# Windowed attention with the values as the stationary operand: the probabilities divided first, the heads left turned, the norm taken by a product with ones

## The reference

```python
lse = jnp.logaddexp(jax.nn.logsumexp(scores, axis=-1), sink)
probs = jnp.exp(scores - lse[..., None])
out = jnp.einsum('bnkgqs,bnskd->bnqkgd', probs, v_band)
...
att = rmsnorm(att, g_att)        # over all 512 attention features of a token
ml = rmsnorm(ml.reshape(b, s, ML_HEADS, ML_V_DIM), ...)
return jnp.concatenate([att, ml], axis=-1) @ w_out
```

## Time and profile before

| | |
|---|---|
| median of 3 runs | 1009.53 us (1009.29 to 1009.66) |
| the profiled execution, its own time | 1009.17 us |
| span of its instructions | 1007.4 us |
| TensorE busy | 997.8 us |
| VectorE busy | 744.7 us |
| ScalarE busy | 505.8 us |
| granted TensorE clock | 0.999 of full |

### The profile page before, as it was taken

How to read it: one execution, slowest core, us unless ns; L and a number is a source line. 1 busy time by engine, 2 the same in 40 slices (tenths; PEclk the granted TensorE clock), 3 DMA queues, 4 the chain that set the end, 5 groups by cost and what they waited for, 6 DMA issues and landing times.

```text
span 1007.4 us, 13062 instructions
## 1 busy us (share of the span) xinstructions
PE 997.8 (99%) x4807; PEld 823.8 (82%) x4807; DVE 744.7 (74%) x1164; ACT 505.8 (50%) x949; POOL 25.9 (3%) x40
## 2 busy tenths in 40 slices
PE   9999999999999999999999999999999999999997
PEld 6788888888888888788888888888888888888886
DVE  4563678875645569997777777777776879996796
ACT  5663448643733225755445445445544634444573
POOL 2000000000300000000000000000000000000000
PEclk9999999999999999999999999999999999999999
DMA  9527554222832241423223223223222999035104
GB/s 343 186 91 224 187 189 168 85 66 108 298 117 84 84 124 51 141 84 105 63 84 104 63 84 104 63 84 100 68 81 81 391 363 336 1 117 190 40 1 167
DMA packets 93255, 133.97 MB, mean 133 GB/s; under 512 B 5884, under 2 KB 56188, under 8 KB 93192
## 3 DMA queue, kind: packets, MB, share of 16 engines
q1 hardware_dynamic: 92808, 132.98, 39.5%
q0 software_dynamic: 96, 0.00, 0.1%
q10 hardware_dynamic: 288, 0.15, 0.1%
HBM read 104.75 MB, written 28.35 MB: 132 GB/s over the span
## 4 chain that ended last, share of the span: by engine, by line
PE 77%; DVE 4%; issue 1%; ACT 0%; DVEq 0%; ACTq 0%
PE pz L2339 7%; PE pz L2340 7%; PE pz L2338 7%; PE pd L2338 6%; PE pd L2339 6%; PE pd L2340 6%; PE pd L2359 4%; PE pd L2362 4%; PE pd L2361 4%; PE pz L2359 3%; PE pz L2362 3%; PE pz L2361 3%; PE pd L2243 3%; PE pd L2245 3%; PE pd L2244 3%; PE pz L2274 1%
## 5 line engine op out<-in xcount | busy, mean ns | idle before, releaser
L1109 ACT ACTIVATE ws_hi<-raw 128x512 fp32r<-128x512 f32 x88 | 52.9, 626 | 102.4 <-PE pz L2340 48.0
L2338 PE MATMUL pz<-ht_hi,ws_hi 128*128 128x512 f32 x240 | 93.7, 390 | 0.2 <-ACT u L1131 0.2
L2340 PE MATMUL pz<-ht_hi,ws_lo 128*128 128x512 f32 x240 | 93.5, 389 | 0.0
L2339 PE MATMUL pz<-ht_lo,ws_hi 128*128 128x512 f32 x240 | 93.4, 389 | 0.0
L2338 PE MATMUL pd<-ht_hi,ws_hi 128*128 128x512 f32 x200 | 78.0, 390 | 0.5 <-DVE u L1792 0.5
L2340 PE MATMUL pd<-ht_hi,ws_lo 128*128 128x512 f32 x200 | 77.9, 389 | 0.0
L2339 PE MATMUL pd<-ht_lo,ws_hi 128*128 128x512 f32 x200 | 77.9, 389 | 0.0
L1809 DVE SCALAR_TENSOR_TENSOR gate<-u,vec,gate 128x1023 f32<-128x1023 f32 (+1 forms) x44 | 56.4, 1283 | 19.4 <-ACT gate L1151 18.6
L1779 DVE TENSOR_TENSOR ws_lo<-raw,ws_hi 128x512 fp32r<-128x512 f32 x88 | 58.5, 686 | 0.8 <-ACT ws_hi L1109 0.7
L1809 DVE SCALAR_TENSOR_TENSOR lift<-u,vec,lift 128x1023 f32<-128x1023 f32 (+1 forms) x44 | 56.2, 1278 | 0.1
L1184 ACT ACTIVATE d_hi<-a 128x512 fp32r<-128x512 f32 x44 | 27.7, 631 | 54.4 <-PE pd L2362 29.6
(11 more groups left out here) (312 smaller groups left out, 2550.8 us busy)
## 6 DMA issues: line engine op xcount, KB each, us to landing
raw<-in_w_up SPq DMA_DIRECT2D x48, 512.0 KB, 5.0
b<-in_w_down SPq DMA_DIRECT2D x49, 256.0 KB, 7.0
act_rows<-gate SPq DMA_DIRECT2D x22, 512.0 KB, 2.6
a<-act_rows SPq DMA_DIRECT2D x44, 256.0 KB, 4.7
w_raw<-in_w_wide SPq DMA_DIRECT2D x16, 512.0 KB, 3.9
x_turned<-in_x_t SPq DMA_DIRECT2D x8, 512.0 KB, 9.5
x_in<-in_x SPq DMA_DIRECT2D x8, 512.0 KB, 12.9
wo_hi_rows<-wo_new_hi SPq DMA_DIRECT2D x8, 512.0 KB, 5.0
```

What stands on the lines that cost most here:

```text
L1109: nc.scalar.activation(ws_hi[m][:, :, :], summand(p, i), ACT.Copy).then_inc(s["ws_hi_made"], 1)
L2338: mm(dst, wh[:, k, :], xh[:, k, :], start=begins and k == 0, stop=False, skip_group_check=not begins)
L2339: mm(dst, wh[:, k, :], xl[:, k, :], start=False, stop=False, skip_group_check=not begins)
L2340: ins = mm(dst, wl[:, k, :], xh[:, k, :], start=False, stop=k == KH - 1, skip_group_check=not begins)
```

## The change

- `attend(n)` takes the values as stationary operand (64 columns for each key/value head) and the turned probabilities as the moving one: two products of 256 columns instead of four of 64. Each writes one half of the partitions; the result has features on the partitions and tokens along the free axis, already turned for the output projection. The rows of `w_out` and of its gain are loaded in the matching order.
- The division by the sum can no longer be made on the result, so ScalarE's `att_p_scale(n)` divides the probabilities (four passes of 128x128) before `turn_probs(n)`, which waits for it; `att_keep(n)` becomes a plain copy.
- `attend(n-4)`, `turn_probs(n-2)` and `attend(n-3)` alternate in step n.
- The norm's sum now runs over partitions. Squares are added pairwise on VectorE (`att_sq_add`, two small sums for a chunk) into one row block, and `att_total` (four products with ones, after `ml_sum(0)`) adds them over the partitions. The root (128x256), its reciprocal on VectorE, a store to memory and a load that spreads it over all partitions follow; VectorE's `att_scale(i)` (128x512) replaces ScalarE's sixteen passes.
- `turn_mix(i)` keeps four of its eight transposes; `mix_high` and `mix_low` work in two halves. `fold` and its three GpSimd instructions are gone. The second tile of the up projection's weights is loaded later.

Left out of this diff: tile and semaphore declarations, waits whose name or count alone changed, the order of `w_out`'s rows.

```diff
@@ -602,8 +601,10 @@
...
             load_gate(0)
-            load_gate(1)
...
+                if i == NT - 1:
+                    sp.wait_ge(s["att_scaled"], NT)
+                    load_gate(1)
@@ -922,14 +916,20 @@
...
+            def att_p_scale(n):
+                _, kw = keys(n)
+                act.wait_ge(s["att_summed"], 2 * n + 2)
+                for j in range(4):
+                    p = probs[:, n % 2, j, 0:kw]
+                    last = nc.scalar.activation(p, p, ACT.Copy, scale=inv[:, n % 4, j:j + 1])
+                last.then_inc(s["att_p_scaled"], 1)
             def att_square(n):
                 act.wait_ge(s["att_kept"], n + 1)
-                if n == 0:
-                    act.wait_ge(s["att_scored"], 5)
-                else:
-                    act.wait_ge(s["att_squared"], n)
-                nc.scalar.activation(att_squares[:, :, :], zq[:, n, :, :], ACT.Square,
-                                     accum_out=sq_att[:, n:n + 1]).then_inc(s["att_squared"], 1)
+                act.wait_ge(s["att_sq_added"], 2 * n)
+                for h, dst in enumerate((att_sq_a, att_sq_b)):
+                    last = nc.scalar.activation(dst[:, :, :], zq[:, n, 2 * h:2 * h + 2, :], ACT.Square)
+                last.then_inc(s["att_squared"], 1)
             def wo_high(k):
@@ -967,9 +967,10 @@
...
                             gate_exps()
-                    for m in (n - 5, n - 4):
-                        if n % 2 == 1 and 0 <= m < NC:
-                            att_square(m)
+                    if 0 <= n < NC:
+                        att_p_scale(n)
+                    if 0 <= n - 5 < NC:
+                        att_square(n - 5)
@@ -993,16 +994,27 @@
...
             def mix_high(i):
-                act.wait_ge(s["mix_turned"], i + 1)
+                act.wait_ge(s["att_scaled"], i + 1)
...
                     act.wait_ge(s["out_done"], 2 * (i - 1))
-                nc.scalar.activation(mix_hi[i % 2][:, :, :].rearrange("p k t -> p (k t)"), pz[1][:, :], ACT.Copy)\
+                nc.scalar.activation(mix_hi[i % 2][:, 0:4, :].rearrange("p j (n t) -> p n j t", n=2),
+                                     zq[:, 2 * i:2 * i + 2, :, :], ACT.Copy).then_inc(s["mix_hi_made"], 1)
+                act.wait_ge(s["mix_turned"], i + 1)
+                nc.scalar.activation(mix_hi[i % 2][:, 4:NK, :].rearrange("p k t -> p (k t)"), bank[2], ACT.Copy)\
...
-            def att_scale(n):
+            def att_root():
+                act.wait_ge(s["att_norm_step"], 1)
+                nc.scalar.activation(att_r[:, :], bank[2][:, 0:2 * P], ACT.Sqrt, bias=eps[:, :],
+                                     scale=1.0 / (ATT_HEADS * HD)).then_inc(s["att_norm_step"], 1)
+            def store_att_row():
...
-                nc.scalar.activation(zq[:, n, :, :], zq[:, n, :, :], ACT.Copy, scale=r_att[:, n:n + 1])\
-                    .then_inc(s["att_scaled"], 1)
+                act.dma_start(att_r_d.rearrange("(g t) -> g t", g=4), att_r[0:P:32, :]).then_inc(s["rows_stored"], 16)
+            def spread_att_row():
+                act.wait_ge(s["rows_stored"], 48)
+                act.dma_start(att_row[:, :], att_r_d.partition_broadcast(P)).then_inc(s["rows_spread"], 16)
             def ml_scale(i):
@@ -1011,12 +1023,12 @@
...
             for i in range(NT):
-                if i == 0:
-                    act.wait_ge(s["att_norm_step"], 1)
-                    nc.scalar.activation(r_att0[:, :], att_sums[:, :], ACT.Sqrt, bias=eps[:, :],
-                                         scale=1.0 / (ATT_HEADS * HD)).then_inc(s["att_norm_step"], 1)
-                    for n in range(4):
-                        att_scale(n)
+                if i == 1:
+                    att_root()
+                if i == 2:
+                    store_att_row()
+                if i == 3:
+                    spread_att_row()
@@ -1024,8 +1036,6 @@
...
                         ml_scale(i - NT + 4)
-                    for n in (2 * i + 2, 2 * i + 3):
-                        att_scale(n)
             def h2_high(i):
@@ -1462,10 +1472,8 @@
...
                     .then_inc(s["att_summed"], 1)
-                dve.wait_ge(s["att_summed"], 3 * n + 1)
-                if n >= 4:
-                    dve.wait_ge(s["att_kept"], n - 3)
-                nc.vector.reciprocal(inv[:, n % 4, :], total1[:, u, :]).then_inc(s["att_summed"], 2)
+                dve.wait_ge(s["att_summed"], 2 * n + 1)
+                nc.vector.reciprocal(inv[:, n % 4, :], total1[:, u, :]).then_inc(s["att_summed"], 1)
             def att_p_keep(n):
@@ -1478,10 +1486,18 @@
             def att_keep(n):
                 dve.wait_ge(s["att_done"], n - n % 2 + 2)
-                dve.wait_ge(s["att_summed"], 3 * n + 3)
-                nc.vector.tensor_tensor(zq[:, n, :, :], bank[7][:, n % 2 * 256:n % 2 * 256 + 256].rearrange("p (j d) -> p j d", j=4),
-                                        inv[:, n % 4, :].unsqueeze(2).to_broadcast([P, 4, HD]), ALU.mult)\
+                c = n % 2 * 256
+                nc.vector.tensor_copy(zq[:, n, :, :], bank[7][:, c:c + 256].rearrange("p (j t) -> p j t", j=4))\
...
+            def att_sq_add(n):
+                dve.wait_ge(s["att_squared"], n + 1)
+                nc.vector.tensor_tensor(att_sq_a[:, :, :], att_sq_a[:, :, :], att_sq_b[:, :, :], ALU.add)\
+                    .then_inc(s["att_sq_added"], 1)
+                dve.wait_ge(s["att_sq_added"], 2 * n + 1)
+                dve.wait_ge(s["att_scored"], min(n + 2, NC))
+                nc.vector.tensor_tensor(z[:, AK, n * CHUNK:(n + 1) * CHUNK], att_sq_a[:, 0, :], att_sq_a[:, 1, :], ALU.add)\
+                    .then_inc(s["att_sq_added"], 1)
             def wo_low(k):
@@ -1580,6 +1596,8 @@
...
                         scale_q((n - 8) // 2)
+                    if 0 <= n - 6 < NC:
+                        att_sq_add(n - 6)
@@ -1591,8 +1609,6 @@
             def ml_carry(i):
                 dve.wait_ge(s["ml_stated"], i + 1)
-                if i == 0:
-                    nc.vector.tensor_copy(att_sums[:, :], bank[7][:, HALF - NC:]).then_inc(s["att_norm_step"], 1)
@@ -1636,7 +1652,13 @@
             def att_norm():
                 dve.wait_ge(s["att_norm_step"], 2)
-                nc.vector.reciprocal(r_att[:, :], r_att0[:, :]).then_inc(s["att_norm_step"], 1)
+                nc.vector.reciprocal(att_r[:, :], att_r[:, :]).then_inc(s["att_norm_step"], 1)
+            def att_scale(i):
+                dve.wait_ge(s["rows_spread"], 16 * 9)
+                v = zq[:, 2 * i:2 * i + 2, :, :]
+                r = att_row[:, i * P:(i + 1) * P].rearrange("p (n t) -> p n t", n=2).unsqueeze(2).to_broadcast([P, 2, 4, CHUNK])
+                nc.vector.tensor_tensor(v, v, r, ALU.mult).then_inc(s["att_scaled"], 1)
             def ml_norm(i):
@@ -1651,9 +1673,12 @@
...
             def mix_low(i):
-                dve.wait_ge(s["mix_hi_made"], i + 1)
-                nc.vector.tensor_tensor(mix_lo[i % 2][:, :, :].rearrange("p k t -> p (k t)"), pz[1][:, :],
-                                        mix_hi[i % 2][:, :, :].rearrange("p k t -> p (k t)").bitcast(F32),
+                dve.wait_ge(s["mix_hi_made"], 2 * i + 1)
+                views = [m[i % 2][:, 0:4, :].rearrange("p j (n t) -> p n j t", n=2) for m in (mix_lo, mix_hi)]
+                nc.vector.tensor_tensor(views[0], zq[:, 2 * i:2 * i + 2, :, :], views[1].bitcast(F32), ALU.subtract)
+                dve.wait_ge(s["mix_hi_made"], 2 * i + 2)
+                nc.vector.tensor_tensor(mix_lo[i % 2][:, 4:NK, :].rearrange("p k t -> p (k t)"), bank[2],
+                                        mix_hi[i % 2][:, 4:NK, :].rearrange("p k t -> p (k t)").bitcast(F32),
...
             def add_x(i, half):
@@ -1726,8 +1751,10 @@
...
                     ml_carry(i + 1)
-                if i == 0:
+                if i == 1:
...
+                if i >= NT - 3 and i < NT - 1:
+                    att_scale(i - NT + 3)
@@ -1738,6 +1765,7 @@
...
                     mix_scale(i + 2)
+                    att_scale(i + 2)
@@ -2108,7 +2136,7 @@
             def turn_probs(n):
                 _, kw = keys(n)
-                pe.wait_ge(s["att_exped"], n + 1)
+                pe.wait_ge(s["att_p_scaled"], n + 1)
@@ -2122,10 +2150,10 @@
...
                 v = att_vb[:, n // 2 - 1, :] if n and n % 2 == 0 else att_va[:, n // 2, :]
-                for j in range(4):
-                    kv = j // 2
-                    ins = mm(bank[7][:, c + j * HD:c + (j + 1) * HD], probs_t[0:kw, n % 2, j, :],
-                             v[0:kw, kv * HD:(kv + 1) * HD], start=True, stop=True)
+                for kv in range(KV_HEADS):
+                    rows = slice(kv * HD, (kv + 1) * HD)
+                    ins = mm(bank[7][rows, c:c + 4 * CHUNK], v[0:kw, rows],
+                             probs_t[0:kw, n % 2, 2 * kv:2 * kv + 2, :].rearrange("k u t -> k (u t)"), start=True, stop=True)
...
             def attention(block):
@@ -2134,13 +2162,12 @@
...
```

(67 more changed lines are left out.)

10 lines of the change are left out of this document (3 added, 7 removed).

## The result

The changed kernel takes 1014.77 us (median of 4 runs, 1014.17 to 1015.42), beside 1009.60 for the kernel before: 1.0048 times as long, 95% interval 1.0036 to 1.0060. The profiled execution took 1014.17, 5.0 more than before; its span is 1012.4. The executions of the kernel before, 1009.29 to 1009.90, and of the changed one do not overlap. I had predicted 1012.7 and slower as the likeliest sign.

What follows compares the result with a forecast made beforehand. TensorE, busy 99% of the span, was taken as the bound. Attention stage +4.8, mLSTM stage +2.0 and `turn_mix` -3.5 gave +3.3 on 1009.17, so 1012.5, stated as 1012.7 us; range 1004.5 to 1015.5.

Steps and rivals of the forecast that it cites:

- the forecast by itself: Whole kernel, the main case: 1012.7 us, by itself 1010.8 to 1014.8; chance 45%.
- TensorE's products: TensorE: two `attend`s take 0.60 us each, saving 0.45 a step; `att_total` adds 0.7, `fold` going saves 0.3.
- the twofold price: `attend` at the skill's 2x speedup: the three steps where TensorE does not wait give another 0.6 us, so 1012.1.
- The weights of step 10: Attention stage: ScalarE's longer chain splits the unit's weights 2.1 to 2.2 us late; 2.1 us lost at step 10.
- Dividing and squares: ScalarE, chunks 7 and 8: four dividing passes (1.26 us) and two squares (0.5), ending at 157.9 and 168.4.
- Step lengths: Attention stage: late copies for `turn_probs` make step 10 last 5.5 us instead of 3.77; steps 12, 14, 16 also lengthen.
- Attention stage: Steps 4 to 18: 6.3 us lost from step 8 to 18, 0.45 won at steps 4 and 6, 0.6 at 18; +4.8.
- mLSTM: mLSTM stage: `ml_state(1)` waits +0.7, wide reciprocal +0.9 or nothing, `att_total` +0.7, `fold` -0.3, `att_scale`s 0; +2.0 us.
- The row: The norm row's store and spread, sharing engines with `w_out`'s loads: taken as 0, up to 7 us if each took 10.1.
- rival 3: Store and spread queue behind `w_out`: 3 to 7 us before mLSTM block 7, 1016 to 1019 us; chance 10%.
- `turn_mix` and the output projection: Four transposes fewer save 0.43 us, eight times, 3.5 in all; output projection's `att_scale` and split are hidden, 0.
- Rivals 1 and 2: Attention stage: slack covers the weights' chain fully (1004.7 us, 20%) or TensorE's losses are about half (1009 to 1010, 25%).

## Why the prediction was right, and where its steps were not

The mechanism came as forecast: TensorE lost its work and got more than that back in waits for w_lo, probs_t and ml_k. The size came at the upper edge, 1014.77 against a band of 1010.8 to 1014.8 for the forecast by itself.

- **TensorE's products.** `attend` 0.58 us, taken as 0.60; steps 4 and 6 won 0.75 and 0.5, taken as 0.45 each. `att_total` 0.64, taken as 0.7. By the Trainium skill (TensorEngine Tiling (Array Packing), "Theoretical Speedup") the swap may be worth up to twofold; this trace shows 0.865 / 0.58 = 1.5, and the first `attend` of a step starts 0.32 us behind the last product of the unit instead of 0.23 (155.54 to 155.86; before, 156.60 to 156.83). The prediction has a slip at the twofold price: three steps that win 0.865 each instead of 0.45, 0.45 and 0.6 give another 1.1, not 0.6, and so 1011.6, not 1012.1.
- **TensorE's busy time** fell by 5.2 us, forecast 6 to 7. At the half clock of step 10 three rows are 0.42, 0.47 and 0.67 us longer than at step 8; without these 1.6 it is 6.8.
- **The weights of step 10.** From the start of step 8 to that of step 10 the changed kernel takes 174.33 - 155.86 = 18.5 us, before 15.0: 3.5 lost, 2.1 forecast. The place, the releaser and the sign were right. The step that failed is the length of ScalarE's chain, where "Dividing and squares" stands twice as a plain sum of passes. The squares also wait for VectorE's additions (0.40 and 1.09), which I had counted on VectorE but not as a wait of ScalarE. The sum and reciprocal of chunk 8, put at 0.55, are 0.45 by the rows that I gave for them. The missed wait also hid which part matters: with it in place, the division is nearly free.
- **Step lengths.** Step 10 lasts 5.3 (forecast 5.5), and steps 12, 14 and 16 0.3, 1.4 and 0.3 us longer than before (0.5, 1.5, 0.5): 3.5 for the four, 4.2 forecast. From step 8 to 18 that makes 3.5 + 3.5 and some 0.4 at the change from each pair of units to `attend` (five times 0.09), 7.4 against 6.3. The longer step 8 (4.4 instead of 4.0) is covered by the loss at 10, as forecast.
- **Attention stage:** +5.8, forecast +4.8.
- **mLSTM.** `ml_state(1)` moved by another 1.1 us (0.7 + 0.7 - 0.3 forecast), the reciprocal took 1.75 us (1.5) and moved `ml_state(3)` by 0.9 (0.9). VectorE's two `att_scale`s were taken as nothing; the first makes `ml_sum(7)` wait 0.45. The second (0.68 us, at 278.85) stands ahead of VectorE's last `ml_t`; GpSimd's product, the last squares and the load of x wait for that one after another, and the load is issued 5.7 us behind the start of `out_project(0)` instead of 5.0. This is read from the order of the rows, not tested. `turn_mix(0)` lies in this stage and gives 0.43 back.
- **The row.** I had named a wait of VectorE for the spread row as a sign of being wrong. It came, with 0.20 us, but rival 3's 3 to 7 us did not: the two transfers took 13 us, and in the run with the narrow reciprocal, where VectorE does not wait for the row, the pass behind `att_scale(0)` begins 275.56 - 273.66 = 1.90 us after the last one ahead of it, in the changed kernel 275.39 - 273.48 = 1.91. What the chain of the page named was a tie.
- **`turn_mix` and the output projection.** -3.5 forecast on the ground that nothing hides the transposes; 2.6 found by putting them back, since two waits of the changed kernel, 0.45 and 0.34, take up part of what they gave. The second is the wait for `mix_lo`, in a stage whose VectorE work I had put at 0.
- **Sum:** +3.3 forecast, +5.0 measured. The terms that I had too small are the chain of step 10 (1.4), the changes to `attend` (0.4), `att_scale(0)` (0.45) and `mix_lo` (0.34); the lengths of steps 10 to 16 were 0.7 too large, and that they took back part of it is luck. Rivals 1 and 2 wanted a cover that was not there; the move of the Sigmoids made it, and the time fell to 1008.25.

What stays open: why the first `att_scale` takes 1.2 to 1.5 us and the second, of the same shape, 0.68.

## What to carry to other kernels

When work is added to a side engine, list the semaphores that it waits for as well as its passes: a short pass that waits for another queue can cost more than a long one that does not, and then leaving out the long one proves nothing. Test a suspected cost twice, with the suspected wait in place and without it. A shorter TensorE program is worth its full gain only after the other engines' order has been fitted to it: the same TensorE work gave 1014.8 us in the order of the change and 1004.0 in another, with the squares on GpSimd.

## What the runs showed of the hardware

- **The clock after a long wait.** Windows of the changed kernel, and of the one with the narrow reciprocal (us, busy times and counts, granted clock in the third column from the end):

```profile
155.00:158.80 3.80, 3.77 (x33) 2.21 (x31) 3.77 (x7) 3.37 (x8) 0.00 (x0) 1.00 0.44 112
174.30:177.00 2.70, 2.67 (x14) 1.20 (x14) 1.65 (x4) 2.24 (x12) 0.94 (x1) 0.63 0.29 108
177.00:179.60 2.60, 2.16 (x22) 2.00 (x21) 2.56 (x6) 2.19 (x7) 0.00 (x0) 0.73 0.73 298
```

```profile
176.00:179.00 3.00, 3.00 (x17) 1.91 (x18) 1.92 (x7) 2.28 (x11) 0.52 (x1) 0.50 0.69 274
179.00:182.00 3.00, 3.00 (x21) 2.60 (x18) 2.41 (x7) 2.11 (x7) 0.00 (x0) 0.69 0.19 75
```

And of the one without the division:

```profile
177.00:179.60 2.60, 1.03 (x17) 0.86 (x17) 2.55 (x6) 0.68 (x3) 0.00 (x0) 1.00 0.85 345
179.60:184.00 4.40, 4.40 (x15) 3.60 (x16) 4.30 (x14) 2.37 (x10) 0.00 (x0) 0.61 0.00 1
```

  After TensorE had waited 2.9 us, the clock was granted at half (1.2 GHz) for a few us: four transposes took 1.08 instead of 0.66. In the changed kernel this lay before a wait for probs_t, which would have ended the step at the same time. In the kernel with the narrow reciprocal it lasted longer and ran into the unit, and `ml_state(0)` came 1.15 us later (251.56 against 250.41): 0.55 of that was there at the start of step 8 already (156.41 against 155.86), the rest came between the starts of steps 10 and 12 (17.05 us against 16.38). That is why that profile's span is no shorter. In the kernel without the division the clock was still full when TensorE began again after 2.9 us; it fell some 5 us later, behind two more waits of 0.35 and 1.57. In the kernels whose longest wait in this stretch was 1.9 us or less the windows from 170 to 182 us show 1.00.
- **The reciprocal on VectorE** takes 0.244 us for 16 columns and 1.75 for 256, 6.3 ns a column, where a pass of 1024 columns takes 1.22 us, 1.2 ns a column.
- **A store of 4 KB** took 5.4 us from issue to landing with `w_out`'s loads in the queues, and ScalarE, which issues both, stood still for 3.1 us of it; no wait of TensorE ends there.
